# A hybrid encoder layer on one Trainium2 core: the order of its start rearranged, with a shorter first choice of experts and earlier gathers of v

## What is computed

```python
xn = rmsnorm(x, norm1);  z = xn @ w_in          # 2888 columns, split in groups
# group A, 4 heads: f = lb + (1 - lb) * sigmoid(af);  S_t = diag(f) S + (1 - f) i^T;  o = S^T silu(aq)
a_out = rmsnorm(o, a_gnorm) * silu(ag)
# group B, 8 heads: index scores choose 64 (68) keys for each query, softmax attention over them
h = x + concat(a_out, b_o) @ w_o
xn2 = rmsnorm(h, norm2);  q = xn2 @ p_wq         # 8 heads
s = two lists of 128 scores a head               # q's halves against p_subkeys
sv, si = top_k(s, 16);  cand = sv[0][:, None] + sv[1][None, :]    # 16 x 16 sums
fv, fi = top_k(cand, 16);  eidx = si[0][fi // 16] * 128 + si[1][fi % 16]
act = gelu(sum(xn2 * p_u[eidx]));  y = h + sum(softmax(fv) * act * p_v[eidx])
```

## Time and profile before

| what | us |
|---|---|
| median of 3 runs | 1270.19 |
| lowest and highest | 1263.31, 1272.36 |
| the profiled execution, its own time | 1266.45 |
| its span (first to last instruction) | 1264.7 |
| busy in the span: PE, DVE, ACT, POOL | 1060.4, 794.4, 356.7, 734.4 |
| DMA | 468.13 MB, mean 370 GB/s |

### The profile page before, as it was taken

One profiled execution on the slowest core, in us unless ns is written; L12 is line 12 of the kernel. 1 busy time (PEld: TensorE's weight loads), 2 busy tenths in 40 slices (PEclk: granted clock), 3 DMA queues, 4 the chain that ended last, 5 costly groups with the idle time before them and its releaser, 6 DMA issues.

```text
span 1264.7 us, 11354 instructions
## 1 busy us (share of the span) xinstructions
PE 1060.4 (84%) x3313; PEld 518.5 (41%) x3313; DVE 794.4 (63%) x1941; ACT 356.7 (28%) x851; POOL 734.4 (58%) x774
## 2 busy tenths in 40 slices
PE   8999989997959988777989799878868777678885
PEld 4766555654326433333543354323223222223231
DVE  1649876989567588877627466666463556563334
ACT  2535215333133342232322333121221221222110
POOL 0005545666656666667656666666666666766654
PEclk9999989998989999989999999999998999999999
DMA  9958989999999999999999999999999999999997
GB/s 379 376 202 278 413 343 367 318 378 409 405 403 408 401 366 391 373 363 366 360 409 409 409 408 383 360 358 410 409 367 348 380 354 371 371 352 371 373 372 293
DMA packets 125629, 468.13 MB, mean 370 GB/s; under 512 B 14072, under 2 KB 17152, under 8 KB 123392
## 3 DMA queue, kind: packets, MB, share of 16 engines
q0 software_dynamic: 110592, 402.70, 83.2%
q1 hardware_dynamic: 14976, 64.70, 13.1%
HBM read 462.86 MB, written 4.42 MB: 369 GB/s over the span
## 4 chain that ended last, share of the span: by engine, by line
PE 43%; DMA 21%; POOL 13%; issue 9%; DVE 8%; another core or an unknown queue 4%; ACT 1%; POOLq 0%; DVEq 0%; SPq 0%; ACTq 0%
PE PSUM L1964 21%; DMA UV<-in_p_v,EIDX 15%; POOL UV L579 7%; PE PSUM L1544 6%; POOL UV L564 6%; DMA UV<-in_p_u,EIDX 5%; PE PSUM L1553 4%; PE PSUM L1743 3%; DVE UV L1461 3%; PE PSUM L1717 2%; PE PSUM L1558 1%; PE PSUM L1565 1%; PE PSUM L1760 1%; DVE SEL L213 1%
## 5 line engine op out<-in xcount | busy, mean ns | idle before, releaser
L1964 PE MATMUL PSUM<-UV,DIAG 128*128 128x512 f32 x1500 | 728.5, 618 | 152.8 <-DMA UV<-in_p_v,EIDX 119.6
L1461 DVE CUSTOM_DVE_ANT_0 UV<-UV,PSUM 128x1024 f32<-128x1024 f32 x384 | 463.6, 1218 | 313.6 <-DMA UV<-in_p_u,EIDX 259.6
L579 POOL DMA_INDIRECT UV<-in_p_v,EIDX x376 | 360.9, 960 | 278.3 <-PE PSUM L1964 140.8
L564 POOL DMA_INDIRECT UV<-in_p_u,EIDX x384 | 364.7, 950 | 237.1 <-issue 108.2
L1964 PEld LDWEIGHTS PSUM<-UV,DIAG 128*128 128x128 f32 x1500 | 267.3, 192 | 552.4 <-issue 274.1
L996 ACT ACTIVATE DIAG<-CST,WGT 128x128 f32<-128x128 f32 x375 | 143.5, 398 | 755.4 <-PE PSUM L1964 408.8
L1544 PE MATMUL PSUM<-WR,XW 128*128 128x512 f32 (+1 forms) x128 | 50.6, 555 | 0.1
L1553 PE MATMUL PSUM<-XW,WR 128*128 128x256 f32 x192 | 46.1, 398 | 3.7 <-issue 3.7
L1553 PEld LDWEIGHTS PSUM<-XW,WR 128*128 128x128 f32 x192 | 38.4, 201 | 12.4 <-issue 6.7
L1544 PEld LDWEIGHTS PSUM<-WR,XW 128*128 128x128 f32 x128 | 24.2, 190 | 25.3 <-issue 22.7
L1461 DVE DVE_READ_ACCUMULATOR2_ANT DOTS<- 128x1 f32 x384 | 31.6, 82 | 0.0
(11 more groups left out here) (286 smaller groups left out, 831.9 us busy)
## 6 DMA issues: line engine op xcount, KB each, us to landing
WR<-in_w_o SPq DMA_DIRECT2D x13, 512.0 KB
UV<-in_p_u,EIDX POOLq DMA_INDIRECT x384
UV<-in_p_v,EIDX POOLq DMA_INDIRECT x384
WR<-in_p_wq SPq DMA_DIRECT2D x10, 512.0 KB
UV<-in_w_o SPq DMA_DIRECT2D x2, 2048.0 KB, 12.1
UV<-in_p_wq SPq DMA_DIRECT2D x2, 2048.0 KB, 9.2
WR<-in_w_B SPq DMA_DIRECT2D x2, 2048.0 KB
UV<-in_w_B SPq DMA_DIRECT2D x4, 512.0 KB, 6.5
```

The costliest lines, as they stand in the source:

```text
L564: nc.gpsimd.indirect_dma_start(UBUF[n % RU], None, a["p_u"], bass.IndirectOffsetOnAxis(EIDX[:, n:n + 1], 0)).then_inc(u_got[n % RU], 16)
L579: nc.gpsimd.indirect_dma_start(VBUF[m % RV], None, a["p_v"], bass.IndirectOffsetOnAxis(EIDX[:, n:n + 1], 0)).then_inc(v_got[m % RV], 16)
L1461: v.tensor_tensor_reduce(out=row, in0=row, in1=XNP, scale=1.0, scalar=0.0, op0=ALU.mult, op1=ALU.add, accum_out=DOTS[:, i % 2, s:s + 1]).t ...
L1964: ins = mm(bank[6 + k][:, :], DIAG[:, m % ND, :], VBUF[m % RV][:, k * 512:(k + 1) * 512], start=False, stop=m % SLOTS == SLOTS - 1 or m == ...
```

## The change

- PE's fillers no longer wait for the identity, and 4 of the 12 become 2 behind the transposes.
- The bounds' product and ACT's exp of it move behind B1 and its copies.
- Silu of AG moves ahead of the copies of the turned probabilities, with a dummy operation ahead of it that loads Silu's table; a dummy square root behind the squares loads Sqrt's.
- In the choices of tile 0, the last keys, the state and the turned x of tile 2 move behind the scores of head 4, the turned x of tile 1 behind those of head 5; both turned x use banks 6 and 7.
- Head 1's choice moves from slot -6 to slot 0 and thus between the first dots; its gate moves too.
- Head 0's first 8 come from the 8 x 8 sums of the first 8 of both lists, before the second 8 of the lists are taken.
- The v buffers are turned by four, so that v0 and v1 lie in w_o's room and v2 to v5 in that of heads 4 to 7. POOL waits for each query's weights alone, and issues v0 to v3 (EARLY = 4) right behind u7.

```diff
@@ -35,7 +35,7 @@
...
 SLOTS = PH * PK
-RU, RV, ND = 8, 6, 6
+RU, RV, ND, EARLY = 8, 6, 6, 4
@@ -79,7 +79,7 @@
 def product_order():
-    o = [("xt", 0, g) for g in range(2)] + [("bp", 0, 0), ("lb",), ("bp", 0, 1), ("rb",), ("bp", 0, 2), ("fp", 0)]
+    o = [("xt", 0, g) for g in range(2)] + [("bp", 0, 0), ("bp", 0, 1), ("lb",), ("rb",), ("bp", 0, 2), ("fp", 0)]
     o += [("ti", 0), ("tk", 0), ("qp", 0)] + [("dt", 0, par, 0) for par in range(2)] + [("tq", 0), ("vp", 0)]
@@ -95,8 +95,9 @@
...
     first = choices(0)
-    beside = first.index(("qq", 0, 3))
-    o += first[:beside] + [("ke", 0), ("u", 0)] + [("xt", t, g) for t in (2, 1) for g in range(2)] + first[beside:]
+    some, more = first.index(("qq", 0, 6)), first.index(("qq", 0, 7))
+    o += first[:some] + [("ke", 0), ("u", 0)] + [("xt", 2, g) for g in range(2)]
+    o += first[some:more] + [("xt", 1, g) for g in range(2)] + first[more:]
     o += [unit_name(*u) for u in UNITS[:8]]
@@ -119,7 +120,7 @@
...
-            b = 8 - 2 * name[1] + name[2]
+            b = 6 + name[2]
         turns[b] += 1
@@ -182,12 +183,12 @@
...
     if t == 0:
-        return 6 * h - 12 if h < 2 else 16 * h - 18
+        return 12 * h - 12 if h < 2 else 16 * h - 18
     return 128 * t + 16 * h - 20
 def gate_slot(t, h):
-    return 4 if (t, h) < (0, 2) else choice_slot(t, h) + 7
+    return 12 if (t, h) < (0, 2) else choice_slot(t, h) + 7
@@ -201,8 +202,8 @@
...
-def top16(own, v, rows, slot, pace):
-    for step in range(5):
+def top16(own, v, rows, slot, pace, steps=range(5)):
+    for step in steps:
         yield slot + step // pace
@@ -303,7 +304,8 @@
...
         UBUF = [UV[:, s * D:(s + 1) * D] for s in range(RU)]
-        VBUF = [UV[:, (RU + s) * D:(RU + s + 1) * D] for s in range(RV)]
+
+        VBUF = [UV[:, (RU + (s + 4) % RV) * D:(RU + (s + 4) % RV + 1) * D] for s in range(RV)]
         SS, CAND = view(UV, (RU + RV) * D, PH, 2, NKEY), view(UV, (RU + RV) * D, PH, PK, PK)
@@ -582,15 +584,22 @@
             take(pool, ("wo", 0, 1))
-            asked = 0
-            for n in range(HEADS * PK):
+            for n in range(RU):
+                if n >= 4:
+                    take(pool, ("qq", 0, n - 4))
+                gather_u(n)
+
+            for n in range(EARLY):
+                if n >= 2:
+                    take(pool, ("qq", 0, n + 2))
+                gather_v(n)
+            asked = RU
+            for n in range(EARLY, HEADS * PK):
                 while asked < min(HEADS * PK, slot_at(max(0, n - RV)) + min(n, RV) + 1):
-                    if asked == 4:
-                        take(pool, ("qq", 0, 3))
                     gather_u(asked)
                     asked += 1
-                if n == 0:
-                    take(pool, ("qq", 0, 7))
+                if n < RV:
+                    take(pool, ("qq", 0, n + 2))
                 gather_v(n)
@@ -776,7 +785,7 @@
...
                     for h in range(PH):
-                        yield 2 if (t, h) < (0, 2) else choice_slot(t, h) + 3
+                        yield 4 if (t, h) < (0, 2) else choice_slot(t, h) + 3
                         act.wait_ge(top_ready, t * PH + h + 1)
@@ -927,10 +936,10 @@
...
             squares(0, X[0], JUNK)
+            out_bp0(0)
+            out_bp1(0)
             act.wait_ge(lb_shift, 1)
             own.done(nc.scalar.activation(SMALLC[:, 16:24], SMALLC[:, 16:24], ACT.Exp), lb_exp)
-            out_bp0(0)
-            out_bp1(0)
@@ -946,10 +955,13 @@
...
+
+            own.done(nc.scalar.activation(SMALLC[:, 73:74], STD1[:, 0:1], ACT.Silu))
+            copy_out(("gp", 0), SG[0], heads4, func=ACT.Silu)
             out_pt(0, 0, 0)
...
             square_o(0)
-            copy_out(("gp", 0), SG[0], heads4, func=ACT.Silu)
+            own.done(nc.scalar.activation(SMALLC[:, 73:74], STD1[:, 0:1], ACT.Sqrt))
             copy_out(("pv", 0), MIXB, heads4)
@@ -966,11 +978,12 @@
...
             first, trunks, gated, gelued = in_slots(choices(0)), in_slots(trunk()), in_slots(gates()), in_slots(gelus())
-            first(CHOICES[0] + 6)
+            first(CHOICES[0] + 12)
             act.wait_ge(id_in, 16)
...
             out_xt(2)
+            first(CHOICES[0] + 14)
             out_xt(1)
@@ -1237,17 +1250,26 @@
...
                 stored(dve, ("se", t, h, 1))
-                yield from top16(own, v, [(SS[:, h, c, :], SV[:, c, :], SIU[:, c, :].bitcast(U32)) for c in range(2)], slot, 5)
+                lists = [(SS[:, h, c, :], SV[:, c, :], SIU[:, c, :].bitcast(U32)) for c in range(2)]
+                if (t, h) == (0, 0):
+
+                    yield from top16(own, v, lists, slot, 5, range(2))
+                    own.caught_up()
+                    own.mark(v.tensor_copy(SIF[:, :, 0:8], SIU[:, :, 0:8].bitcast(U32)))
+                    few = SCORE[:, 0:64]
+                    own.done(v.tensor_tensor(few.rearrange("p (i j) -> p i j", i=8), wide(SV[:, 0, 0:8], 2, 8), wide(SV[:, 1, 0:8], 1, 8), ALU.add))
+                    own.done(v.max(FV[:, 0:8], few))
+                    own.done(v.max_index(FI[:, 0:8].bitcast(U32), FV[:, 0:8], few))
+                    yield from decode(t, h, 0, 8, slot + 1, 3)
+                    yield from top16(own, v, lists, slot, 5, range(2, 5))
+                else:
+                    yield from top16(own, v, lists, slot, 5)
                 yield slot + 1
...
-
-                    own.done(v.max(FV[:, 0:8], row))
-                    own.done(v.max_index(FI[:, 0:8].bitcast(U32), FV[:, 0:8], row))
-                    yield from decode(t, h, 0, 8, slot + 1)
                     own.done(v.match_replace(out=row, in_to_replace=FV[:, 0:8], in_values=row, imm_value=PICKED))
@@ -1257,20 +1279,20 @@
...
-            def decode(t, h, lo, hi, slot):
-
-                k, n = slice(lo, hi), hi - lo
-                own.mark(v.tensor_scalar(FPART[:, 0, k].bitcast(U32), FI[:, k].bitcast(U32), 4, None, ALU.logical_shift_right))
-                own.mark(v.tensor_scalar(FPART[:, 1, k].bitcast(U32), FI[:, k].bitcast(U32), PK - 1, None, ALU.bitwise_and))
+            def decode(t, h, lo, hi, slot, bits=4):
+
+                k, n, j = slice(lo, hi), hi - lo, slice(0, 1 << bits)
+                own.mark(v.tensor_scalar(FPART[:, 0, k].bitcast(U32), FI[:, k].bitcast(U32), bits, None, ALU.logical_shift_right))
+                own.mark(v.tensor_scalar(FPART[:, 1, k].bitcast(U32), FI[:, k].bitcast(U32), (1 << bits) - 1, None, ALU.bitwise_and))
                 own.caught_up()
                 own.done(v.tensor_copy(FPF[:, :, k], FPART[:, :, k].bitcast(U32)), top_ready if hi == PK else None)
-                iota = wide(wide(IOTA, 1, n), 1, 2)
-                own.done(v.tensor_tensor(OH[:, :, k], wide(FPF[:, :, k], 3, PK), iota, ALU.is_equal))
+                iota = wide(wide(IOTA[:, j], 1, n), 1, 2)
+                own.done(v.tensor_tensor(OH[:, :, k, j], wide(FPF[:, :, k], 3, 1 << bits), iota, ALU.is_equal))
                 if n == PK:
                     yield slot + 1
-                own.done(v.tensor_tensor(OH[:, :, k], OH[:, :, k], wide(SIF, 2, n), ALU.mult))
-                own.done(v.tensor_reduce(EPART[:, :, k], OH[:, :, k], axis=AX, op=ALU.add))
+                own.done(v.tensor_tensor(OH[:, :, k, j], OH[:, :, k, j], wide(SIF[:, :, j], 2, n), ALU.mult))
+                own.done(v.tensor_reduce(EPART[:, :, k], OH[:, :, k, j], axis=AX, op=ALU.add))
                 at = slice((t * PH + h) * PK + lo, (t * PH + h) * PK + hi)
@@ -1883,20 +1905,20 @@
...
-            pe.wait_ge(id_in, 16)
...
             idle(8)
+            pe.wait_ge(id_in, 16)
             pe.wait_ge(x_in[0], 16)
...
                 transposes(("xt", 0, g), [X[0][:, (4 * g + c) * P:(4 * g + c + 1) * P] for c in range(4)])
-            idle(4)
+            idle(2)
             stored(pe, ("xt", 0, 0))
             rows_of(("bp", 0, 0), XNT2, weights("B0"))
+            rows_of(("bp", 0, 1), XNT2, weights("B1"))
             pe.wait_ge(lb_in, 16)
...
             end(nc.tensor.transpose(pb[:, 0:8], LBRAW, IDENT[0:8, 0:8]), ("lb",))
-            rows_of(("bp", 0, 1), XNT2, weights("B1"))
@@ -1941,10 +1963,11 @@
...
             first, trunks = in_slots(choices(0)), in_slots(trunk())
-            first(CHOICES[0] + 5)
+            first(CHOICES[0] + 11)
             last_keys(0)
...
             turned_x(2, X[2])
+            first(CHOICES[0] + 13)
             turned_x(1, X[1])
```

## The result

The changed kernel takes 1284.76 us (median of four, 1283.73 to 1288.22); the kernel before, in the same comparison, 1269.64 (1263.31 to 1272.36). The ratio is 1.0131, 95% interval 1.0088 to 1.0174: 15 us slower, where 3.2 faster was forecast, and outside the forecast's range of 1258 to 1272. The profiled execution of after took 1288.22 us (span 1285.5). In this and all later comparisons executions marked as slow are left out (two: e1's 1280.98 and e4's 1371.89).

The account below looks back on a forecast made before the run. PE's chain to about 286 us was taken to set the end, then the DMA's stream of gathers. Start 2.8 plus silu 0.4, all else 0, made 3.2 us: 1263.3 profiled, 1267.0 against the median; range 1258 to 1272.

Parts of the forecast that it names:

- The bound and the chain: PE's chain to v's sums at 173.89 us sets the end; bringing PE earlier brings the end earlier by as much.
- rival A: Gathers count, not PE: the whole early fill is kept, a gain of 8.0 us, to 1262.2; chance 0.12.
- The start: Fillers without the identity wait bring B0 3.5 us earlier and AF from 28.9 to 26.1: 2.8 us gained.
- the silu: Silu sooner in ACT, with a dummy behind the squares loading Sqrt, ahead of w_o's product: 0.4 us gained.
- The bounds' chain: Bounds' product, exp and scaling of x, behind B1, end at 25.6, 0.5 us under AF's 26.1: cost 0.
- the 2.8: The start's gain in us, carried through the first tile to the silu, as PE follows AF at fixed distance.
- rival C: PE's clock stays at the lower level through B0 at the start: 3.5 us slower, 1273.7; chance 0.08.
- The failed step: Short first lists, second head's choice between dots: first gather at 94.2, first dot 12 us sooner, worth 0.
- the early v rows: Four gathers of v issued behind u7 fill DMA time at 100 to 115 us; worth 0.
- The order ... I take 0: Tile 0's choices, last keys and turned x reordered: taken as 0, between 1.6 us gained and 3.3 lost.
- Rival D: ACT's pause of 3.34 us falls where PE waits for it and eats the 3.2 gained: 1270.2; chance 0.16.
- Rival B: PE's stall in the last two long products goes, 7.6 us more: gain 10.8, to 1259.4; chance 0.14.

Follow-up runs that it names:

- e1: Changed kernel with the old order of tile 0's choices, last keys and turned x put back; 1276.96 us, ratio 1.0034 to the kernel before.
- e4: Kernel before with only the edits of the start and the silu; 1271.77 us, ratio 1.0009 to the kernel before.
- e9: Changed kernel again, unaltered, on a chip of the slower kind; 1286.23 us, ratio 1.0120 to the kernel before.
- e12: Kernel before with at most 4 gathers outstanding in its first 41, slower kind; 1265.51 us, ratio 0.9968 to the kernel before.
- e13: Kernel before with 64 already met waits of PE added ahead of the long products, faster kind; 1204.06 us.
- e15: Changed kernel, unaltered, on a chip of the faster kind; 1196.77 us, ratio 0.9984 to the kernel before.
- e2: Changed kernel without the four early gathers of v (EARLY = 0); 1279.18 us, ratio 1.0079 to the kernel before.
- e11: Changed kernel with at most 6 gathers outstanding in the first 41, slower kind; 1279.82 us, ratio 1.0072 to the kernel before.
- e18: Changed kernel with at most 5 gathers outstanding in its first 41, faster kind; 1197.62 us, ratio 0.9995 to the kernel before.
- e5: Changed kernel with at most 4 gathers outstanding in the first 41, faster kind; 1203.25 us, ratio 1.0031 to the kernel before.
- e3: Changed kernel with the second head's choice put back ahead of the first dot; 1274.23 us, ratio 1.0018 to the kernel before.
- e8: Kernel before with at most 4 gathers outstanding throughout, faster kind; 1443.87 us, ratio 1.2050 to the kernel before.
- e10: Changed kernel with at most 4 gathers outstanding in the first 41, slower kind; 1265.41 us, ratio 0.9972 to the kernel before.
- e14: Changed kernel with at most 5 gathers outstanding in its first 41, faster kind; 1197.35 us, ratio 0.9991 to the kernel before.
- e16: Kernel before with 64 already met waits of PE added ahead of the long products, faster kind; 1203.29 us.
- e17: Kernel before with 64 already met waits of PE added ahead of the long products, faster kind; 1203.10 us.

## Why the prediction was wrong

**The bound and the chain: right for what comes later, not shown for a small gain.** PE's way to v's sums sets the end nearly one for one where it gets longer: 21.3 us of it in e9 against e12 are 20.7 of time, and 4.85 in e13 are 4.9. That what brings PE earlier "brings the end earlier by as much" is not borne out on the slower kind: e4's 3.2 us brought nothing that its interval shows, e12's 6.9 brought 3.8. So the 3.2 might not have shown at the end there even without the crawl. Gathers that come earlier without PE were not worth rival A's 8.0 us: after issues its first at 94.39 (94.2 forecast) and is slower, and e15, where nothing crawls, gains 2.0.

**The start: right, term by term.** B0 at 6.90 (forecast 6.7), AF at 26.25 (26.1), w_o's product at 70.00 (69.7); the silu gave 0.33 (0.4), by the distance from AF to w_o's product, 44.08 before and 43.75 after. Of the fourteen profiled runs with the new start AF began in thirteen between 26.05 and 27.04, in e2 at 27.43. In after the scaling of x ended at 26.10, where 25.6 was forecast, and was last. The bounds' chain itself was costed right (5.2 us from B1's end): B1 ended at 20.87 and not at 20.4. The exp's table load took 1.28 us and the exp began 0.02 later (22.26, 23.56), so again nothing shows of the drain of 1.38 us that the page "ScalarE: Activation LUTs" of the Trainium skill adds in "What ACT_TABLE_LOAD costs". What was missed: the 2.8 don't always carry through the first tile. From AF to the first query product it is 59.6 us in ten of the fourteen profiled runs with the new start, 61.2 in three (e11, e15, e18) and 62.8 in e5; in these four the granted clock falls to the lower level for a part of 50 to 58 us (mean 0.79 in e15, above, 1.00 in after). In the six with the old start it is always 59.9. The clock did fall, as rival C feared, but at another place and for 1.6 us (3.2 in e5) instead of 3.5. At B0, where C put it, it did not fall in after: the products of B0 and B1 took 13.97 us together, and B0's alone 7.03 before. Why it falls in 4 of 14 was not tested.

**The failed step: "All of this is DVE's and POOL's, and neither is on PE's chain at this place", "worth 0".** It priced the earlier gathers by who waits for them, and not by what they do to an engine that waits for none of them. The new order, the early v rows and the early first dot together give POOL an unbroken run of 25 issues over PE's and ACT's short steps; on the slower kind the long products then start 21.6 us later than before, when 3.2 earlier was forecast, and the kernel takes 15 us more. Each of e1, e2 and e3 breaks or moves a part of the overlap and takes back part of the stage's 24.5 us (13.2, 8.7 and 11.7). No rival had a kernel slower by this way, and over 1% slower was given 0.02. The same stands against the "0" of the early v rows and against "The order ... I take 0": its bounds, -1.6 and +3.3, came from one pause of ACT. On the faster kind the order is worth 0 as forecast: the stage takes 26.4 us in e15 and in e8, which has the old order.

**Rival D named it and had the size wrong.** ACT's pause "falls where PE waits for it" is what happened, but not as one pause of 3.34: there are seven between 99 and 131, 27.4 us together. One pause of about 3 us stays with at most four gathers outstanding (2.97 in e12, 3.73 in e10), and none shows in e13, e14 or e15. The row was a sample of a state that belongs to the slower kind, not a price.

**Rival B came true too.** The 64 records took 13.98, as worked out (13.9). It gives back 7.6 of 21.6, which leaves the 14.0 measured at v's sums and 15 at the end. "It comes with a full DMA, and the DMA will be as full" was wrong for after, where the share is 0.42 from 180 to 190. That this is why the stall stayed away is not shown: in e3 the same 64 records run in 13.98 from 162.25, with 411 GB/s from 165 to 170 and 406 from 170 to 175. What the page "Runtime: NRT & Kernel Launch" of the Trainium skill says in "Instruction fetch mechanics" of fetches, that they are mostly hidden, could not be tried on the stall, since e13, e16 and e17 found none to shift. For the crawl the trace of after has this: between 90 and 128 us the queues that the profile calls "instruction" move one packet, from 102 to 104, while PE has eight waits (7.50, 4.96 and six shorter), so they are not a fetch each.

**What stays open.** Why PE and ACT crawl. It grows with the gathers outstanding, or with the fuller DMA that comes with them (e10 and e11 against e9), and needs the slower kind of chip (e15). The stall at the same record in before and e4 hints at a place in PE's instructions, and no run here shows it. On the faster kind, where the crawl is absent, the change brings 2.0 us (0.7 to 3.1 by the interval) of the forecast's 3.2. In e15's profile the fall of the clock took 1.6; whether the other executions lose as much, their mean clocks (0.981 to 0.988, 0.987 in the profiled one) don't tell.

**Is there a better version?** e10 and e12 both beat the kernel before on the slower kind, by 3.9 and 3.8 us of 1269.26, and the changed one by more; the upper ends of their intervals, 0.9994 and 0.9992, are barely below 1. On the faster kind e10's kernel costs 0.3% (e5), and the changed kernel without a limit (e15) has the lowest time, not told apart from a limit of five (e14, e18).

## What to carry to other kernels

Ask of every transfer that a change brings forward what else runs while it is in flight, and not only who waits for it. A pause of an issuing queue may be what lets a stage of short dependent steps beside it run at full pace; look at which engines show "remote" or "issue" waits during unbroken runs of gathers, and treat one such wait as a sample of something that can grow with the overlap. Run the unaltered kernel on the same chip as the remedy before you call a cause shown: e5 to e8 looked like proof until e15.

## What the runs showed of the hardware that was not expected

- Two kinds of chips: the kernel before takes 1269 to 1271 us on one and 1198.6 to 1199.1 on the other, 6% apart; the changed kernel moves 379 GB/s from 800 to 1000 us in after and 410 in e15.
- On the slower kind PE makes its short steps 0.7 to 2.1 us apart and ACT pauses for up to 8.62 us while POOL issues gathers without a break; DVE's dots (1.22 us each) and POOL's issues (0.94) keep their pace. The same kernel on the faster kind shows nothing of it.
- Four outstanding gathers of 512 KB are too few for the stream (322 GB/s against 408 on the faster kind, the time 20% up). In the first 41 gathers alone, a limit of four makes the changed kernel 0.3% slower than the kernel before on the faster kind, and on the slower one 1.6% faster than without the limit.
- 64 waits that are already met cost PE 3.15 us, 0.05 each, and its granted clock falls behind them (mean 0.90 from 120 to 130 us in e13), which costs 1.7 us more.
